# Seven block products in place of eight for two 512-column stretches of feed-forwards 2 to 4, with the sums of weights made by accumulating DMAs

## What is computed

```
def swiglu(h, w_in, w_out):
    g, u = split_cols(h @ w_in, (D_FF, D_FF))      # D_FF = 2816
    return (jax.nn.silu(g) * u) @ w_out
...
x = x + 0.5 * swiglu(rms_norm(x, g[0]), ffn1_w_in[layer], ffn1_w_out[layer])
... a mixer, then a cross-attention over mem ...
x = x + 0.5 * swiglu(rms_norm(x, g[4]), ffn2_w_in[layer], ffn2_w_out[layer])
```

## Time and profile before

| | |
|---|---|
| median of 3 runs | 1624.25 us (1623.36 to 1624.75) |
| the profiled execution's own time | 1623.05 us |
| its span | 1621.8 us |
| PE (TensorE) busy | 1595.5 us, 98% |
| DVE (VectorE) busy | 1109.3 us, 68% |
| ACT (ScalarE) busy | 861.6 us, 53% |
| POOL (GpSimd) busy | 227.5 us, 14% |
| moved by DMA | 295.22 MB, 182 GB/s over the span |

### The profile page before, as it was taken

The page is one execution under the profiler, slowest core; times in us unless marked ns, Lnnn a source line. Parts: engine busy times, 40 slices in busy tenths (PEclk is TensorE's granted clock), DMA queues, the critical chain, the costliest instruction groups (busy, mean ns, idle before and its releaser), DMA issues.

```text
span 1621.8 us, 21203 instructions
## 1 busy us (share of the span) xinstructions
PE 1595.5 (98%) x8050; PEld 1331.2 (82%) x8050; DVE 1109.3 (68%) x1769; ACT 861.6 (53%) x1324; POOL 227.5 (14%) x351
## 2 busy tenths in 40 slices
PE   8999999999999999999999999999999999999998
PEld 6888877788888888888889888888889877888886
DVE  6775788867655556555596775655568997776566
ACT  5554556855545445444555555544454457454444
POOL 2499901000000000000000000000014442100000
PEclk9999999999999999999999999999999999999999
DMA  9766656445455565655654553555685554556563
GB/s 283 242 208 213 207 169 191 150 142 156 140 185 188 188 186 178 191 185 190 213 171 156 163 186 111 183 187 187 189 261 166 165 157 143 182 194 193 188 188 109
DMA packets 187543, 295.22 MB, mean 182 GB/s; under 512 B 13510, under 2 KB 108144, under 8 KB 186160
## 3 DMA queue, kind: packets, MB, share of 16 engines
q1 hardware_dynamic: 183264, 275.93, 54.4%
q0 software_dynamic: 3888, 17.60, 3.4%
q10 hardware_dynamic: 288, 0.33, 0.1%
HBM read 288.29 MB, written 5.25 MB: 181 GB/s over the span
## 4 chain that ended last, share of the span: by engine, by line
PE 86%; DVE 8%; ACT 3%; issue 2%; POOL 1%; DMA 0%; SPq 0%; DVEq 0%; ACTq 0%
PE b L445 25%; PE b L447 24%; PE b L446 24%; PE b L667 4%; DVE wlo L1677 2%; PE b L669 2%; ACT whi L1118 1%; PE b L690 1%; PE b L920 1%; PE b L902 1%; PE b L511 1%; PE b L527 1%; PE b L611 1%; PE b L564 1%; ACT R L1207 1%
## 5 line engine op out<-in xcount | busy, mean ns | idle before, releaser
L1677 DVE TENSOR_TENSOR wlo<-raw,whi 128x1024 fp32r<-128x1024 f32 (+1 forms) x523 | 648.7, 1243 | 430.6 <-ACT whi L1118 429.2
L1118 ACT ACTIVATE whi<-raw 128x1024 fp32r<-128x1024 f32 (+1 forms) x523 | 549.8, 1053 | 554.3 <-PE b L447 518.4
L445 PE MATMUL b<-whi,hT 128*128 128x512 f32 (+1 forms) x1040 | 413.0, 397 | 9.4 <-DVE wlo L1677 8.2
L447 PE MATMUL b<-whi,hT 128*128 128x512 f32 (+1 forms) x1040 | 404.8, 389 | 0.0
L446 PE MATMUL b<-wlo,hT 128*128 128x512 f32 (+1 forms) x1040 | 404.3, 389 | 0.0
L445 PE MATMUL b<-whi,oT 128*128 128x512 f32 x672 | 265.1, 394 | 0.0
L447 PE MATMUL b<-whi,oT 128*128 128x512 f32 x672 | 262.0, 390 | 0.0
L446 PE MATMUL b<-wlo,oT 128*128 128x512 f32 x672 | 261.6, 389 | 0.0
L445 PEld LDWEIGHTS b<-whi,hT 128*128 128x128 f32 x1040 | 195.8, 188 | 54.7 <-DVE wlo L1677 10.4
L447 PEld LDWEIGHTS b<-whi,hT 128*128 128x128 f32 x1040 | 195.7, 188 | 41.6
L446 PEld LDWEIGHTS b<-wlo,hT 128*128 128x128 f32 x1040 | 196.0, 188 | 37.7
(11 more groups left out here) (349 smaller groups left out, 1855.9 us busy)
## 6 DMA issues: line engine op xcount, KB each, us to landing
raw<-in_ffn_w_in SPq DMA_DIRECT2D x350, 256.0 KB, 3.2
raw<-in_ffn_w_out SPq DMA_DIRECT2D x88, 512.0 KB, 3.4
raw<-in_w_ff SPq DMA_DIRECT2D x64, 512.0 KB, 4.0
raw<-in_w_in SPq DMA_DIRECT2D x36, 512.0 KB, 3.7
raw<-in_x_w_kv SPq DMA_DIRECT2D x32, 512.0 KB, 4.1
raw<-in_even_w_in SPq DMA_DIRECT2D x24, 512.0 KB, 4.2
raw<-in_odd_w_in SPq DMA_DIRECT2D x24, 512.0 KB, 4.0
raw<-in_x_w_q SPq DMA_DIRECT2D x16, 512.0 KB, 4.1
```

The source lines that it names most:

```text
L445: T.matmul(out, ah, bh, start=start, stop=False, skip_group_check=skip)
L447: return T.matmul(out, al, bh, start=False, stop=stop, skip_group_check=skip)
L1118: E.activation(K.whi[j % NSPLIT][:, 0:n], K.raw[j % NRAW][:, 0:n], ACT.Copy).then_inc(*S.whi.done(j))
L1677: V.tensor_tensor(K.wlo[j % NSPLIT][:, 0:n], K.raw[j % NRAW][:, 0:n], K.whi[j % NSPLIT][:, 0:n].bitcast(F32), ALU.subtract).then_inc(*S.wl ...
```

## The change

For chunks 3 and 4, and for chunks 6 and 7, of f1, f2 and f3, the product of 256 rows by two 512-column halves (the 512 gate columns and the 512 up columns of two chunks) is made as one 2 x 2 block product by Winograd's form of Strassen's scheme. With A11, A12, A21, A22 the quarters of h (128 rows by 512 k) and B11 to B22 the quarters of w_in (512 k by 512 columns; B11 and B21 up, B12 and B22 gate), seven products P1 to P7 of 128 x 512 x 512 take the place of eight. Such a stretch is called a block here; there are six, each with 14 pieces of w_in, of six matmuls each, in place of 8 pieces of 12. Its parts:

- Four sums of activation quarters (S1 to S4) are made on VectorE in `R2` in chunk 1 and split into `mT` in chunk 2 (`activation_sums`, `row_sums`). The memory's split moves from chunks 5 and 6 of f1 to chunks 9 and 10 of f2.
- Four sums of weight quarters (T1 to T4), two tiles each, are made in `R1`. SyncE loads B11 or B22 (six tiles for a block, `tile_load`), from `TILE_LEAD = 6` pieces before the block on, and GpSimd adds to them with ten accumulating DMAs (`block_sums`). T2 takes two additions one after the other, and T4 is T2 plus B21, once VectorE has split T2.
- ScalarE and VectorE split all 14 pieces: six are quarters that come through the `raw` ring (B11, B21, B22), eight are sums in `R1`.
- VectorE joins the products (`joined`): five additions of 128 x 512 from PSUM for each block. ScalarE copies P1 out of PSUM (`snapped`). The silu and the product with the up part are 128 x 512 twice, in place of 128 x 256 four times.
- The rows of w_out of chunk c-1 stand after P7 and after P3; those of the block's two chunks, four pieces, follow in the next chunk.

```diff
-    Ffn("f1", 32, 0, "ffn2_w_in", "ffn2_w_out", 2816, True, 0.5, "x0"),
+    Ffn("f1", 32, 0, "ffn2_w_in", "ffn2_w_out", 2816, True, 0.5, "x0", (3, 6)),
...
+PRODUCTS = (("P1", 4, 1, "B11"), ("P6", 5, 1, "T2"), ("P5", 6, 1, "T1"), ("P2", 4, 0, "B21"), ("P7", 5, 0, "T3"),
+            ("P3", 6, 0, "B22"), ("P4", 5, 0, "T4"))
+TILES = (("T1", "B11"), ("T2", "B11"), ("T3", "B22"))
+TILE_LEAD = 6
...
+        def block(c):
...
+            for q, (name, bank, opens, of) in enumerate(PRODUCTS):
+                if name == "P2":
+                    pe.wait_ge(*S.snapped.at(key))
+                elif name == "P7":
+                    pe.wait_ge(*S.joined.at((*key, "U2")))
+                elif name == "P3":
+                    pe.wait_ge(*S.joined.at((*key, "V")))
+                elif name == "P4":
+                    pe.wait_ge(*S.joined.at((*key, "G1")))
...
+                for h in range(2):
...
+                    pe.wait_ge(*S.wlo.at(j))
+                    hi, lo = K.split_views(j)
+                    for kk in range(2):
+                        ins = products(banks[bank][:, :], K.factor(name, 2 * h + kk), (hi[:, kk, :], lo[:, kk, :]),
+                                       bool(opens) and h == kk == 0, h == kk == 1, True)
...
+                for _ in range(shares[q]):
+                    p, kk = last_row.pop(0)
+                    down(p, [kk])
+            free[4] = (S.product.at((f.name, c, 0)),)
+            free[5] = (S.joined.at((*key, "U1")),)
+            free[6] = (S.joined.at((*key, "G0")),)
...
+            reached(3)
+            dve.wait_ge(*S.snapped.at(key))
+            joined("U2", "P6", 5, K.fs[0], K.fs[2])
+            reached(5)
+            joined("V", "P5", 6, K.fs[0], K.fs[1])
+            reached(9)
+            dve.wait_ge(*S.joined.at((*key, "V")))
+            joined("G1", "P7", 5, K.fs[1], K.fs[1])
+            reached(11)
+            dve.wait_ge(*S.joined.at((*key, "U2")))
+            joined("G0", "P3", 6, K.fs[2], K.fs[2])
+            reached(12)
+            dve.wait_ge(*S.dense.at((*key, "P2")))
+            gated(0, banks[4][:, :])
+            reached(13)
+            joined("U1", "P4", 5, K.fs[0], K.fs[0])
+            dve.wait_ge(*S.joined.latest())
+            gated(1, K.fs[0])
...
+    def block_sums(f):
...
+                E.dma_start(K.tile[i].rearrange("p (k n) -> p k n", k=2),
+                            D[f.w_in][f.l, k0 * P:(k0 + 2) * P, c0:c0 + 512].rearrange("(k p) n -> p k n", p=P),
+                            accum_op=ALU.add).then_inc(*S.tile_sum[i].done((*key, total or name + of), step=16))
+            for name, total in (("T1", "T1"), ("T2", None), ("T3", "T3")):
+                for h in range(2):
+                    add(name, "B12", h, S.tiled[f.slot(c, name, h)].at((*key, name)), total)
+            for h in range(2):
+                add("T2", "B22", h, S.tile_sum[f.slot(c, "T2", h)].at((*key, "T2B12")), "T2")
+            for h in range(2):
+                add("T4", "B21", h, S.wlo.at(K.at[b, 2 + h]), "T4")
...
+    for n, j in enumerate(K.rings):
+        name, l, k0, nk, cols = K.plan[j]
+        while tiles and K.at[f"{tiles[0][0].name}b{tiles[0][1]}", 0] - TILE_LEAD + tiles[0][2] <= j:
+            tile_load(*tiles.pop(0))
```

More of the change, by code:

```diff
@@ L136, in __init__ @@
         S.x_turned = tuple(s[f"xt{i}"] for i in range(5))
+        S.tiled = tuple(s[f"tile{i}"] for i in range(8))
+        S.tile_sum = tuple(s[f"sum{i}"] for i in range(8))
         S.masks, S.cst, S.columns, S.mem_turned, S.sm, S.bl, S.mem, S.rel, S.cl, S.gf, S.cum, S.dec = (
@@ L168, in memory @@
         self.xv = R2[:, 2048:4096].rearrange("p (t n) -> p t n", t=2)
+        self.tile = [R1[:, 1024 * i:1024 * i + 1024] for i in range(8)]
         self.vsb = sb("vsb", [P, 2, 512])
@@ L246, in gain, with operand, activation, factor @@
         return self.gcol[:, i:i + 1]
+    def operand(self, j):
+        kind, of, i = self.source[j]
+        return self.raw[of % NRAW] if kind == "ring" else self.tile[i]
+    def activation(self, f, c, t):
+        c0 = f.begin(c)
+        return self.fa[(2 * c0 + t) % 4][:, 256 * (c - c0):256 * (c - c0) + 256]
+    def factor(self, name, kt):
+        if name in ("P1", "P2", "P4"):
+            k, t = kt + 4 * (name != "P1"), int(name == "P4")
+            return tuple(a[:, k, P * t:P * t + P] for a in self.hT)
+        at = 512 * ("P5", "P6", "P7", "P3").index(name) + P * kt
+        return tuple(a[:, :, :].rearrange("p k t -> p (k t)")[:, at:at + P] for a in self.mT)
     def split_views(self, j):
@@ L288, with __init__ @@
 class Ffn:
-    def __init__(self, name, g0, l, w_in, w_out, F, gated, scale, before):
+    def __init__(self, name, g0, l, w_in, w_out, F, gated, scale, before, blocks=()):
+        self.blocks = blocks
         self.name, self.g0, self.l, self.w_in, self.w_out = name, g0, l, w_in, w_out
@@ L298, in k0, with begin, slot, quadrant @@
         return self.per * (c % self.slots)
+    def begin(self, c):
+        return c - 1 if c - 1 in self.blocks else c
+    def slot(self, c, of, h):
+        return {"T1": 0, "T3": 2}.get(of, 6 if self.blocks.index(c) % 2 else 4) + h
+    def quadrant(self, c, of, h):
+        return (4 if of[1] == "2" else 0) + 2 * h, 256 * c + (0 if of[2] == "2" else self.F)
+    def units(self):
+        return [c for c in range(self.nch) if c - 1 not in self.blocks]
+    def ahead_of(self, c):
+        return [] if c == 0 else [c - 2, c - 1] if c - 2 in self.blocks else [c - 1]
 def downs(f, c):
@@ L437, in piece @@
         j = len(K.plan)
+        K.source.append(("ring", len(K.rings), None))
+        K.rings.append(j)
         K.plan.append((name, l, k0, nk, tuple(cols)))
@@ L722, in ffn @@
         last, groups = f.nch - 1, range(f.per // 2)
-        for c in range(f.nch):
+        for c in f.units():
+            if c in f.blocks:
+                block(c)
+                continue
             if c:
-                beside = {2 if f.before is None and c == 1 else 0: lambda: turn(c - 1)}
+                beside = {n: lambda p=p: turn(p) for n, p in enumerate(f.ahead_of(c))}
+                if f.before is None and c == 1:
+                    beside = {2: lambda: turn(0)}
                 if f.before is None and c == 1:
@@ L1254, in down, with block, behind, opened @@
                 weights(K.first[f.name, "row", chunk, rows[-1]] + AHEAD)
+        def block(c):
+            b, key, y = f"{f.name}b{c}", (f.name, c), K.stat(("-y", f.name), 2)
+            def behind(o):
+                weights(K.at[b, o] + 1 + AHEAD)
+            def opened(t, gate):
+                act.wait_ge(*S.joined.at((*key, gate)))
+                s = K.fs[2 - t]
+                E.activation(s, s, ACT.Silu, scale=y[:, t:t + 1]).then_inc(*S.silu.done((f.name, c, t)))
+            for o, p in enumerate(f.ahead_of(c)):
+                behind(o)
+                high(p)
+            behind(1)
+            act.wait_ge(*S.dense.at((*key, "P1")))
+            act.wait_ge(*S.product.at((f.name, c - 1, 1)))
+            E.activation(K.fs[0], banks[4][:, :], ACT.Copy).then_inc(*S.snapped.done(key))
+            behind(9)
+            opened(1, "G1")
+            behind(11)
+            opened(0, "G0")
+            weights(K.at[b, 13] + AHEAD)
+        def row_sums(i):
+            at = slice(1024 * i, 1024 * i + 1024)
+            act.wait_ge(*S.row_summed.at((f.name, i)))
+            E.activation(K.mT[0][:, :, :].rearrange("p k t -> p (k t)")[:, at], K.R2[:, 2048 + 1024 * i:3072 + 1024 * i],
+                         ACT.Copy).then_inc(*S.shi.done((f.name, i)))
         last, groups = f.nch - 1, f.per // 2
-        for c in range(f.nch):
+        for c in f.units():
+            if c in f.blocks:
+                block(c)
+                continue
             for p in pieces(f"{f.name}up{c}"):
@@ L1259, in ffn @@
                     silus(0)
-                if c and p == (3 if f.before is None and c == 1 else 1):
-                    high(c - 1)
+                for n, chunk in enumerate(f.ahead_of(c)):
+                    if p == (3 if f.before is None and c == 1 else 1 + n):
+                        high(chunk)
+                if f.blocks and c == 2 and p in (0, 1):
+                    row_sums(p)
                 if c == 0 and p == 1 and f.before:
@@ L1979, in ffn @@
         last, groups = f.nch - 1, f.per // 2
-        for c in range(f.nch):
+        for c in f.units():
+            if c in f.blocks:
+                block(c)
+                continue
             for p in pieces(f"{f.name}up{c}"):
-                if c and p == (3 if f.before is None and c == 1 else 1):
-                    low(c - 1)
+                for n, chunk in enumerate(f.ahead_of(c)):
+                    if p == (3 if f.before is None and c == 1 else 1 + n):
+                        low(chunk)
+                if f.blocks and c == 1:
+                    activation_sums(p)
+                if f.blocks and c == 2 and p in (1, 2):
```

(1 more changed line is left out.)

133 lines of the change are left out of this document (111 added, 22 removed).

## The result

The changed kernel takes **1704.5 us** (median; 1703.5 to 1707.2), the kernel before 1624.5 (1623.4 to 1626.9) beside it: ratio 1.0495, 95% interval 1.0483 to 1.0507. The profiled execution spans 1702.3 us, so 80.5 us came in where the forecast had 1.7.

What follows compares the result with a forecast made beforehand. TensorE was taken as the bound. A block: -2.72 us for matmuls, +0.5 and +1.5 for VectorE, +1.0 for late additions, +0.28; six blocks +1.7 us, so 1626 us, with 8 in 10 for 1612 to 1685.

Steps and rivals of the forecast that it cites:

- the lower one: GpSimd's additions on the DMA engines: each costs one plain transfer, 1.30 us; T2 1.0 us late a block, between 0 and 2.6.
- rival 2: Each addition takes the DMA engines for two transfers; TensorE waits at P6 for T2, +9.3 us a block, 1680 us; chance 0.27.
- VectorE's terms: VectorE's joins and products in a block make TensorE wait: 0.5 us early and 1.5 at the end, 2.0 of 2.72 back.
- Twelve matmuls less: TensorE, each block: 84 matmuls of w_in for 96, at 0.227 us each, 2.72 us saved, 16.3 us in all.
- VectorE's order: Order of splits, joins and products on VectorE in a block: 2.0 us lost, between 0 and 3.2.
- U1: Join at the block's end: TensorE's next chunk waits for bank 5, 1.05 us more.
- the product: Product of t = 0 at the block's end: comes 0.45 us too late for bank 4, wanted by the next chunk's first piece.
- U2 and V: Joins between two splits in a block's first ten pieces: 0.37 us for U2 and 0.13 for V, 0.5 us.
- Activation sums: VectorE's adds, low parts and other operations in chunks 1 and 2 of each feed-forward: hidden in idle time, cost 0.
- GpSimd's issue of a DMA: Ten DMAs a block at 0.55 us each, 5.5 us on an otherwise idle queue: cost 0.
- The sums on the edges: Forecast's own range 1621 (no lateness) to 1640 us (2.6 late, 3.2 lost on VectorE); rival 2 decides from about 1.1 transfers an addition.
- Wrong if TensorE waits at P6 for more than 3 us: Sign against the forecast: a longer TensorE wait at P6 of a block; additions on time would show no idle time there.

Runs made afterwards that it cites:

- the kernel with both moves: Against the kernel without additions (1626.2 us): at a block's end the bank 5 join goes ahead of the last low half, last activation sum made in chunk 2; 1615.2 us.

## Why the prediction was wrong

**The failed step** is the price of an addition on the DMA engines. The prediction took "the lower one, to which the only GpSimd load of this size is nearest", one transfer. Measured: 2.94 us against 1.44 for the same load without the addition, so two. The nearest row by form (a load from GpSimd) lacked what the addition is inferred to have, the read of the tile; the store's row had it, and its price was right. With it the prediction's own working gives rival 2, whose mechanism came true: 12.4 us lost a block in f1, by the stretches above, where rival 2 had 10, and 1704.5 where it had 1680. The Trainium skill (Collectives: The Full Stack, "The bandwidth ceiling: the fold count and why AG ≠ RS ≠ AR") has two source reads for the add of a collective's reduce; the ratio 2.04 agrees.

**What rival 2 left out**, 24 us. 6 of them are VectorE's terms (1626.2 without additions, where -0.7 a block makes 1620), 18 are lateness, 78 us in place of 60. It counted lateness only at P6, but chunks 2 and 5 pay as well, for the ring's pieces (74 us of ScalarE's waits), and TensorE restarts slowly, below. By the matmuls' starts in f1 to f3, 80 of the kernel after, with no wait before them, come 0.38 to 0.47 us after the one before, 16 us beyond the pace in all; in the kernel without additions one does. These 16 us can't be set against the 18 one to one, since the DMA engines go on meanwhile and later waits get shorter.

By the other steps:
- Twelve matmuls less, -2.72 us a block: the pace holds, 0.227 us.
- VectorE's order: 2.0 us a block predicted. A block's stretch would be 26.4 us by 114 matmuls of 0.2265 and 0.55 for transposes; without additions it is 28.8 to 29.1, so 2.4 to 2.7. Of it 1.07 are U1, as predicted (1.05), about 0.4 the product (0.45), and 1.1 stay in the kernel with both moves. Some 0.4 of these stand at P2's first tile, where the prediction had 0.5 for U2 and V, and 0.3 still at the next chunk's first piece.
- Activation sums: 0 predicted, 2.2 us in all three measured. The slack was taken as a sum over a chunk, where the operations stand in a row ahead of chunk 1's products; moved by one place they cost nothing.
- GpSimd's issue of a DMA: 0.55 us predicted, 1.20 measured for an accumulating one (median of the 60), hidden all the same.
- The sums on the edges: by the prediction's own terms the range goes from 1620 to 1643, not 1621 to 1640, and the engines are full from 0.96 transfers an addition on, not 1.1. So its lower bound of one transfer stood already at the edge.
- "Wrong if TensorE waits at P6 for more than 3 us": it waited 6.95.

## What to carry to other kernels

A DMA that adds into a tile cost the DMA engines two transfers here: count it so before the sum, and bound an unknown operation by the row that has its parts, not its name. Engine time is then a budget over a stretch, not over the transfer: 60 additions bunched ahead of their use cost 78 us, and 30 cost nothing once they started early, one came every three pieces and their sum stayed under what the stretch holds; with 36 of them and two blocks a feed-forward the kernel is 0.5% faster than before. A load that waits in an in-order queue for a tile still in use holds up what stands behind it. An engine's slack is of use only where it stands: the same GpSimd addition was free in a plain chunk and cost 1.9 us in a block.

## What the hardware showed that was not expected

TensorE's granted clock fell in waits and stayed low after them. One-microsecond windows of the kernel after, in f1 (the number ahead of the DMA share is the clock):

```profile
478.00:479.00 1.00, 0.00 (x0) 0.00 (x0) 0.42 (x1) 0.54 (x1) 0.00 (x0) 1.00 1.02 393
479.00:480.00 1.00, 0.14 (x1) 0.15 (x1) 1.00 (x2) 0.00 (x0) 0.94 (x2) 0.85 1.05 408
480.00:481.00 1.00, 1.00 (x3) 0.81 (x4) 0.94 (x1) 0.92 (x1) 1.00 (x3) 0.50 1.09 383
...
482.00:483.00 1.00, 1.00 (x3) 0.72 (x3) 1.00 (x3) 0.81 (x1) 0.69 (x1) 0.50 1.10 252
483.00:484.00 1.00, 1.00 (x6) 0.81 (x4) 1.00 (x2) 0.00 (x0) 0.00 (x0) 0.94 1.11 256
484.00:485.00 1.00, 1.00 (x6) 0.83 (x5) 0.31 (x1) 0.00 (x0) 0.00 (x0) 1.00 1.10 268
...
498.00:499.00 1.00, 1.00 (x4) 0.81 (x3) 0.00 (x0) 0.19 (x1) 0.62 (x1) 0.50 0.24 86
```

It fell during a wait of 2.1 us, stood at 0.50 (1.2 GHz) until 483, and then came back to 1.00 (2.4 GHz); matmuls start every 0.43 us in place of 0.227 meanwhile. After the 7 us wait at P6 the same happens: 0.50 in the window from 498 to 499, and starts at 497.84, 498.27, 498.69. So these waits cost more than their length: 3 us at 0.50 are 1.4 us of work lost. The waits of 0.5 and 0.7 us at the end of a block, in the kernel without additions, left the clock at 1.00.
